# A decoder layer's prologue by tiles of 128 of the model width: x, adaLN weights and the first projections on one core

## The reference, cut to what matters

```python
mod = jax.nn.silu(c) @ w_ada + b_ada            # c (1, 1024), w_ada (1024, 3072)
shift, scale, gate = jnp.split(mod, 3, axis=-1)
h = x * (1.0 + scale[:, None, :]) + shift[:, None, :]
proj = h @ w_in + b_in                          # w_in (1024, 6664)
# split into sb_q, sb_k, sb_v, sb_z | ml_q ... ml_z | ml_i, ml_f (4 + 4 columns) | merge gates
```

## Time and profile before

| | us |
|---|---|
| median of 3 runs | 1022.5 (1020.33 to 1023.93) |
| the profiled execution | 1021.37 |
| its span, first to last instruction | 1019.6 |
| PE busy in the span | 955.2 (94%) |
| DVE busy | 600.2 (59%) |
| ACT busy | 456.5 (45%) |
| POOL busy | 177.3 (17%) |
| DMA | 73.64 MB, mean 72 GB/s |
| mean granted TensorE clock | 0.975 |

### The profile page before, as it was taken

One profiled execution on the slowest core, in us unless ns is written; L12 is line 12 of the kernel. 1 busy time (PEld: TensorE's weight loads), 2 busy tenths in 40 slices (PEclk: granted clock), 3 DMA queues, 4 the chain that ended last, 5 costly groups with the idle time before them and its releaser, 6 DMA issues.

```text
span 1019.6 us, 14219 instructions
## 1 busy us (share of the span) xinstructions
PE 955.2 (94%) x4965; PEld 765.9 (75%) x4965; DVE 600.2 (59%) x1100; ACT 456.5 (45%) x811; POOL 177.3 (17%) x145
## 2 busy tenths in 40 slices
PE   3399999999999999999999999999999999988995
PEld 2367877888877888778888778788788888866883
DVE  2854785665795655765648857543653332264766
ACT  1133465654465563656554656534743222251221
POOL 1101022322022330132420233211100000002220
PEclk9689998999999999999999999999999999999998
DMA  8702111111211102201112111125712211332232
GB/s 290 249 11 68 44 51 42 33 32 31 93 41 32 40 21 62 72 21 51 30 32 93 36 27 42 32 52 181 242 48 67 51 41 41 94 109 97 83 109 97
DMA packets 78083, 73.64 MB, mean 72 GB/s; under 512 B 4792, under 2 KB 66360, under 8 KB 78044
## 3 DMA queue, kind: packets, MB, share of 16 engines
q1 hardware_dynamic: 73116, 58.31, 20.0%
q0 software_dynamic: 2624, 8.54, 2.5%
q10 hardware_dynamic: 2304, 6.29, 1.6%
HBM read 64.59 MB, written 8.40 MB: 72 GB/s over the span
## 4 chain that ended last, share of the span: by engine, by line
PE 82%; DVE 10%; issue 2%; ACT 2%; DMA 2%; SPq 1%; POOL 0%; DVEq 0%; ACTq 0%; POOLq 0%
PE bank L618 42%; PE bank L598 9%; PE bank L599 9%; PE bank L600 9%; PE bank L731 3%; PE bank L715 3%; PE bank L704 1%; DVE m_q L1522 1%; DMA x_rows<-in_x 1%; DMA a_raw<-in_w_ada 1%; PE bank L744 1%; DVE a_acc L1295 1%; DVE m_q L1534 1%; DVE m_w L1546 1%; PE bank L687 1%
## 5 line engine op out<-in xcount | busy, mean ns | idle before, releaser
L618 PE MATMUL bank<-hH,wH 128*128 128x512 f32 x704 | 282.3, 401 | 0.7 <-DVE wL L1309 0.7
L618 PE MATMUL bank<-hL,wH 128*128 128x512 f32 x704 | 280.3, 398 | 0.0
L618 PE MATMUL bank<-hH,wL 128*128 128x512 f32 x704 | 276.2, 392 | 0.0
L557 POOL TENSOR_TENSOR ez<-ez,rem 128x512 f32<-128x512 f32 (+3 forms) x96 | 139.2, 1470 | 415.4 <-DVE rem L1471 415.4
L1309 DVE SCALAR_TENSOR_TENSOR wL<-w_raw,wH 128x512 fp32r<-128x512 f32 (+1 forms) x122 | 90.8, 748 | 150.7 <-ACT wH L896 149.9
L618 PEld LDWEIGHTS bank<-hH,wH 128*128 128x128 f32 x704 | 132.9, 189 | 39.9 <-issue 10.7
L618 PEld LDWEIGHTS bank<-hH,wL 128*128 128x128 f32 x704 | 133.1, 189 | 27.6
L618 PEld LDWEIGHTS bank<-hL,wH 128*128 128x128 f32 x704 | 133.1, 189 | 25.4 <-issue 1.0
L896 ACT ACTIVATE wH<-w_raw 128x512 fp32r<-128x512 f32 (+1 forms) x122 | 75.5, 620 | 108.7 <-PE bank L600 75.2
L1471 DVE TENSOR_TENSOR_SCAN rem<-rem,ones 128x512 f32<-128x512 f32 (+3 forms) x96 | 88.6, 965 | 39.0 <-ACT rem L981 39.0
L968 ACT ACTIVATE ez<-bank 128x512 f32<-128x512 f32 (+3 forms) x96 | 41.9, 489 | 97.2 <-PE bank L706 97.2
(11 more groups left out here) (234 smaller groups left out, 1458.3 us busy)
## 6 DMA issues: line engine op xcount, KB each, us to landing
w_raw<-in_w_in SPq DMA_DIRECT2D x104, 256.0 KB, 2.9
a_raw<-in_w_ada SPq DMA_DIRECT2D x16, 512.0 KB, 4.8
x_rows<-in_x SPq DMA_DIRECT2D x8, 512.0 KB, 7.2
raw<-in_w_ada POOLq DMA_DIRECT2D x8, 512.0 KB, 5.6
x_in<-in_x SPq DMA_DIRECT2D x8, 512.0 KB, 4.2
out_y<-res SPq DMA_DIRECT2D x8, 512.0 KB, 2.9
raw<-in_w_out SPq DMA_DIRECT2D x10, 256.0 KB, 4.5
m_w<-bm_scratch ACTq DMA_DIRECT2D x4, 512.0 KB, 4.3
```

The source lines that it names most:

```text
L557: g.tensor_tensor(e, e, r, ALU.mult).then_inc(a_done[h], 1)
L618: ins = t.matmul(proj_ps[half][:], w, a, start=(r == 0), stop=(r == JOB_MM // 2 - 1))
```

## The change

All loads of the prologue but the parameters are cut by 128 columns of the model width. For tile d SP loads a column block of x (`x_rows[:, :, cols_d]`, 1024 pieces of 512 bytes, 512 KB) and column blocks of the shift and scale parts of `w_ada` (two loads of 1024 pieces of 512 bytes). `a_raw` has 3 buffers of one tile each. Weight chunks 0 to 5 are now gate rows, q and k for tiles 0 to 3 (g = 0, 1, 2) and 4 to 7 (g = 3, 4, 5); their split parts have buffers of their own (`w_proH`, `w_proL`). Chunks 6 to 9 (v and z) are as they were.

Per tile d, DVE accumulates `ada_rows(d)` (8 instructions of 256 columns), PE sums (`ada_columns(d)`, 4 matmuls of one column), DVE makes the two columns of `mod`, PE transposes the x tile (`turn_x(d)`, 8 transposes), ACT reads the bank with scale and bias applied (`shifted(d)`, two instructions, and a third for `hH`), DVE makes `hL` (`low_h`, one iteration later), and PE adds the tile to gate rows, q and k (`tile_of`, 18 matmuls). DVE's old pass over `xT` and its copies out of PSUM are gone. Jobs v and z follow whole. The eight DMAs of the gate rows go from POOL to SP, behind the last prologue chunk. The pieces below belong to SP, to PE, to ACT and, the last two, to DVE:

```diff
+            for d in range(KT):
+                cols_d = slice(d * P, (d + 1) * P)
+                sp.dma_start(x_rows[:, :, cols_d], x_v[:, :, cols_d]).then_inc(x_cols_in[d], 16)
+                if d >= A_BUFS:
+                    sp.wait_ge(ada_used, KT * (d - A_BUFS + 1))
+                for what in range(2):
+                    sp.dma_start(a_raw[:, d % A_BUFS, :, what], w_ada_w[:, :, what, cols_d])\
+                        .then_inc(a_in[d % A_BUFS], 16)
+                if d == 0:
+                    for g in range(3):
+                        pro_load(g)
+                elif d < 4:
+                    pro_load(d + 2)
+            for g in range(PRO_CHUNKS, 2 * PRO_JOBS):
                 pro_load(g)
-            for n in range(2 * KT):
-                k, what = divmod(n, 2)
-                if n >= 4:
-                    sp.wait_ge(ada_used, n - 3)
-                sp.dma_start(a_raw[:, n % 4], w_ada_v[:, k, what * D:(what + 1) * D]).then_inc(a_in[n % 4], 16)
-            for g in range(3, 2 * PRO_JOBS):
-                pro_load(g)
+            sp.wait_ge(rows_zero, 5)
+            for half in range(2):
+                sp.wait_ge(drained[half], 1)
+            for q in range(4):
+                sp.dma_start(r_f[32 * q:32 * q + NH, :], r_if[NH:2 * NH, :]).then_inc(rows_in, 16)
...
+            ada_columns(0)
+            for d in range(KT):
+                turn_x(d)
+                if d:
+                    tile_of(d - 1, 0, PRO_K - 1)
+                if d + 1 < KT:
+                    ada_columns(d + 1)
+                if d:
+                    tile_of(d - 1, PRO_K - 1, PRO_K)
+            tile_of(KT - 1, 0, PRO_K)
+            pe.sem_inc(w_first_used, PRO_K)
+            for n in range(PRO_K, PRO_JOBS):
+                project(0, 0, JOB_MM, base_job=n, other_banks=1 if n == PRO_K else 0)
...
+            def shifted(d):
+                act.wait_ge(mod_done, 2 * d + 2)
+                if d > 1:
+                    act.wait_ge(hL_done, d - 1)
+                for n in range(2):
+                    act.wait_ge(m_filled[n], d + 2 - n)
+                    a.activation(h_raw[:, d % 2, halves(n)], misc_ps[n][:], ACT.Identity, scale=mod[:, 1, d:d + 1],
+                                 bias=mod[:, 0, d:d + 1]).then_inc(m_drained[n], 1)
+                for n in range(2):
+                    act.wait_ge(m_drained[n], d + 2 - n)
+                a.activation(hH[:, d], h_raw[:, d % 2], ACT.Copy).then_inc(hH_done, 1)
             for g in range(3):
                 pro_split(g)
             for d in range(KT):
-                act.wait_ge(h_full, d + 1)
-                a.activation(hH[:, d], xT[:, d], ACT.Copy).then_inc(hH_done, 1)
-                if d == 5:
-                    pro_split(3)
+                shifted(d)
+                if d < 6:
+                    pro_split(d + 3)
...
             for d in range(KT):
+                ada_rows(d)
+                mod_columns(d)
                 if d == 0:
-                    mod_columns(0, 0, ADA_FIRST)
-                if d == ADA_FIRST:
-                    mod_columns(1, ADA_FIRST, KT)
-                if d == 0:
-                    dve.wait_ge(m_drained[1], 8)
-                v.tensor_scalar(xT[:, d], xT[:, d], mod[:, 1, d:d + 1], mod[:, 0, d:d + 1], ALU.mult, ALU.add)\
-                    .then_inc(h_full, 1)
-                if d:
+                    for g in range(3):
+                        pro_split(g)
+                else:
                     low_h(d - 1)
-                if d == 6:
-                    pro_split(3)
+                if d and d < 7:
+                    pro_split(d + 2)
             low_h(KT - 1)
...
+            row_logs()
+            pro_split(PRO_CHUNKS + 3)
+            row_columns()
+            for g in range(2 * PRO_JOBS, 2 * PRO_JOBS + 2):
+                pro_split(g)
```

More of the change, by code:

```diff
@@ L124 @@
 PRE = 48
-ADA_FIRST = 3
+PRO_K = 3
+PRO_CHUNKS = 2 * PRO_K
+A_BUFS = 3
 def segments():
@@ L366, in build_kernel @@
         M_PRO, M_PER = [10, 9], [20, 20]
+        pro_ps = [[y_ps[0:2 * NH, :], misc_ps[2][0:2 * NH, :]],
+                  [proj_ps[half][:] for half in range(2)], [z_ps[half][:] for half in range(2)]]
+        ada_ps = misc_ps[0]
         F_V, F_MK, F_MV, F_CHUNK, F_HN = 0, 1, 2, 3, 19
@@ L641, in _, with ada_columns @@
-            for d in range(KT):
-                if d == 0:
-                    pe.wait_ge(ada_used, 2 * KT)
-                for what in range(2):
[L645 to L649, removed]
+            def ada_columns(d):
+                pe.wait_ge(ada_used, KT * (d + 1))
+                pe.wait_ge(m_drained[0], d + 1)
+                for what in range(2):
+                    for part in range(2):
+                        ins = t.matmul(ada_ps[:, what:what + 1], a_acc[:, d % 2, part, what],
+                                       ones[:, 0:1], start=part == 0, stop=part == 1)
+                ins.then_inc(ada_done, 1)
@@ new lines, in tile_of @@
+            def tile_of(k, first, last):
+                pe.wait_ge(hL_done, k + 1)
+                if k % 4 == 0:
+                    pe.wait_ge(wL_done, PRO_K * (k // 4 + 1))
+                for n in range(first, last):
+                    w = [z[:, PRO_K * (k // 4) + n, k % 4, 0:P if n else 2 * NH] for z in (w_proH, w_proL)]
+                    for half in range(2):
+                        ins = split_product(pro_ps[n][half], w, (hH[:, k, halves(half)], hL[:, k, halves(half)]),
+                                            k, KT)
+                        if k == KT - 1:
+                            ins.then_inc(filled[half], 1)
@@ L880, in _ @@
             a.preload_act_table_set("natural_log_exp_and_others")
[L883 to L889, removed]
+            act.wait_ge(cols_done, 1)
+            a.activation(small[:, 0:KT], cols[:, ROW_C:ROW_C + KT], ACT.Exp, scale=-1.0).then_inc(c_exp, 1)
             def split_high(slot, loads, freed, scale=1.0, width=P):
@@ L943, in _ @@
                     g = 2 * n + 3 + half
[L944 to L950, removed]
+                    if PRO_CHUNKS + 3 <= g < 2 * PRO_JOBS + 2:
+                        pro_split(g)
+                if n == 2:
                     act.wait_ge(rows_in, 16 * 8)
@@ L1285, in _, with ada_rows @@
             dve.wait_ge(silu_done, 1)
[L1287 to L1304, removed]
+            def ada_rows(d):
+                dve.wait_ge(a_in[d % A_BUFS], 32 * (d // A_BUFS + 1))
+                if d > 1:
+                    dve.wait_ge(ada_done, d - 1)
+                for k in range(KT):
+                    acc, row = a_acc[:, d % 2, k % 2], a_raw[:, d % A_BUFS, k]
+                    if k < 2:
+                        v.tensor_scalar(acc, row, silu_c[:, k:k + 1], None, ALU.mult).then_inc(ada_used, 1)
+                    else:
+                        dve.wait_ge(ada_used, KT * d + k - 1)
+                        v.scalar_tensor_tensor(out=acc, in0=row, scalar=silu_c[:, k:k + 1], in1=acc,
+                                               op0=ALU.mult, op1=ALU.add).then_inc(ada_used, 1)
             def split_low(slot, number, scale=1.0, width=P):
@@ L1313, in pro_split @@
             def pro_split(g):
[L1314 to L1318, removed]
+                if g < PRO_CHUNKS:
+                    n = g % PRO_K
+                    columns = P if n else 2 * NH
+                    dve.wait_ge(wH_done, g + 1)
+                    v.scalar_tensor_tensor(out=w_proL[:, g, :, 0:columns], in0=w_raw[:, g % 3, :, 0:columns],
+                                           scalar=SB_SCALE if n == 1 else 1.0, in1=w_proH[:, g, :, 0:columns],
+                                           op0=ALU.mult, op1=ALU.subtract).then_inc(wL_done, 1)
+                else:
+                    split_low(g % 3, g + 1)
```

125 lines of the change are left out of this document (50 added, 75 removed).

## The result

The changed kernel takes 1029.12 us (median of 10 runs, 1025.95 to 1031.51), the kernel before beside it 1021.21 (10 runs, 1018.53 to 1023.93): ratio 1.0077, 95% interval 1.0063 to 1.009. The forecast was 1012.5. Its profiled execution has a span of 1027.4 us, 7.8 more than before. Two launches of the kernel before that were timed beside the first four experiments were slow, 1210.28 and 2426.31 us; the ratios leave them out.

What follows compares the result with a forecast made beforehand. PE was taken as the bound, so an earlier prologue shifts everything: chunk 6 lands at 49.2, 28.7 to the last tile, 22.0 for v and z, `gate_columns` at 100.6 instead of 110.6, hence 1012.5 us; range 1006 to 1022.5.

Steps and rivals of the forecast that it cites:

- all behind it is unchanged and moves with it: Everything behind the start of `gate_columns` keeps its length, so that start's 10.0 us gain passes whole to the kernel.
- Who waits for whom: Prologue lists: ACT, then DVE, then PE wait for weight chunk 6, so streaming by tiles runs for tiles 0 to 3 only.
- The block: ACT's `pro_split(6)` behind `shifted(3)` waits for chunk 6 until 49.2 us; ACT idles near 9 us, PE from 43 to 53.
- The price of the loads: Prologue loads in 512-byte pieces run at 329 GB/s, so 13.89 MB up to chunk 6 take 42.2 us.
- The bound of 275: Lower bound on the load rate in GB/s: chunk 6 lands 8.3 us later, leaving a gain of 1.7 us.
- SP's own waits don't stretch it: SP's waits while issuing prologue loads don't delay chunk 6's landing at 49.2: each `ada_rows(1)` to `(4)` ends with two tiles queued.
- The rounds behind the block: DVE's rounds after chunk 6's splits: 6.1 us, then 7.1, with `ada_rows(7)` done at 66.6.
- 12 slow matmuls (5.1) ahead of its sums: In the second round after chunk 6, PE's lower-clock matmuls precede its sums, making that round 7.1 us.
- Rival 3: PE stays at the lower clock between the tile stage's short bursts: 16 us late, 1028 us; chance 0.04.
- The gate rows' path: Gate rows complete at 75.2, through bias, DMAs, Exp, Ln and `row_logs` to split 9 at 92.2; PE waits 0.7 us.
- rival 4: No stall in the prologue, or its gain eaten by hand-offs or load price: within 3 us of before; chance 0.12.
- the case of 395 GB/s: Prologue loads at big-piece rate: chunk 6 lands at some 44.5 us, limited by DVE's pace; gain 14.7 us.

Runs made afterwards that it cites:

- the first four experiments: Kernel before with 48 do-nothing instructions on PE, or 34 on DVE; changed kernel with PE's, or DVE's, loop head aligned: 1021.73, 1027.17, 1025.64, 1029.01 us.

## Why the prediction was wrong

It said 10 us faster, 0.73 on faster; the kernel is 8 us slower, outside the range. Two steps failed: "all behind it is unchanged and moves with it" (item 6, some 8 us), and the time of the last tile, which made the prologue's gain vanish (items 2 to 5, 9.9 us).

1. **Who waits for whom: right.** The block is where it was put, with its releasers, the idle stretch on PE and the fallen clock. Taking it away brought 16 us: the rounds of 5.96 us run on while the loads arrive, and PE keeps its clock.
2. **The price of the loads: mis-sized.** 329 GB/s came from a stretch of 1.5 us; steady, the stream gives 290. 13.89 MB at 290 are 47.9 us and not 42.2: 5.7 of the 7.0 us by which the block ended late. The bound of 275, which came from the packets' own busy time, was nearer than either direct rate.
3. **"SP's own waits don't stretch it": false.** It looked only at the `w_ada` buffers. Chunk 3's wait for DVE's first split held SP 3.6 us, and the rate from 15 to 20 us was 222 GB/s. What remains of the 7.0, 1.3 us, I put to this: 5 us at 222 and not at 290 lose 1.2. That share wasn't measured alone.
4. **The rounds behind the block: PE's part mis-sized.** The last `ada_rows` ends at 76.0, 19.8 after the block, where 17.4 were forecast. The steps on DVE were right (2.46 and 0.62 for `ada_rows`, 1.22 for `low_h`). Two terms of PE were not. "Four are 0.9" for `ada_columns` counts records as products: the 32 of the earlier trace rows are 16 sums, so four sums are 8 records and take 1.87 us at the lower clock, 0.95 at the upper. With that the first round took 6.8 and not 6.1. And the 7.1 of the second has "12 slow matmuls (5.1) ahead of its sums", while PE's list has 18 there and the transposes. The timeline of PE has the missing third of tile 3 from 62.21 to 64.92, then the transposes, then the 12:

```profile
62.21 0.77 PE L613 MATMUL bank<-hH,w_proH 128*128 128x512 f32 x1
...
64.92 1.91 PE L662 MATMUL bank<-ident,x_rows 128*128 128x128 f32 x8
66.48 0.78 PE L613 MATMUL bank<-hH,w_proH 128*8 128x512 f32 x1
...
70.17 0.95 PE L650 MATMUL bank<-ones,a_acc 128*128 128x1 f32 x8
```

   `ada_rows(6)` had ended at 67.25, so DVE waited for PE, and the round took 8.8. The clock was not the reason: it was back at about 68 us (0.50, 0.50 and 0.67 in the windows above), and the 12 matmuls took 3.7 us and not the 5.1 that the forecast had. Rival 3 had no part in it.
5. **From the last `ada_rows` on: half a us late.** It is 34.5 us to `gate_columns`, where 34.0 were forecast, and this is PE's: the 36 matmuls of tiles 6 and 7 took 8.45 us and not 8.1. The gate rows' path was 1.1 us longer than forecast up to Exp, since SP's eight small issues took 5.0 us and not 3.0, from 85.87 on:

```profile
85.87 2.58 SPq L458 DMA_DIRECT2D r_f<-r_if  x4
88.49 2.44 SPq L460 DMA_DIRECT2D r_i<-r_if  x4
```

   Split 9 ended at 101.96, and PE waited for it 0.55 us, where I had 0.7. That the two agree is luck: the sum of this path slipped (82.2 + 2.1 + 6.5 are 90.8 and not 91.5), and without the slip no wait was forecast.
6. **What the sum lacked: the returns.** Items 2 to 5 bring `gate_columns` from 100.6 to 110.5 (7.0 + 2.4 + 0.5), which is the time of rival 4, "no gain", though with the block in place. The step that turned that into a loss was "all behind it is unchanged and moves with it". The instructions are the same ones, but in another place of their lists, and that alone costs 8 to 9 us. Nothing in the sum priced the lists' length, though the page of before shows queues of kind instruction and the diff shows that both lists grow. With that cost taken away the changed kernel takes 1020.07 us: inside the stated range, but with a gain of 0.5 us and not of 10.
7. **A slip that decided nothing.** In the case of 395 GB/s, 38.5 + 3.4 + 1.9 are 43.8 and not 44.5.

## What to carry to other kernels

When a change adds instructions ahead of a long loop, compare the return of that loop in both traces (idle time ended by "issue", blocks in the queues of kind instruction) before judging the change itself: an alignment of the loop's head separates the two, and here it was worth 0.9%. Ask of each wait in a hand-written order what lies behind it in the same list: a split that isn't due for 30 us stood ahead of the tiles and cost 16 us. Price a stream by a row of the same kind that is long enough to be steady, and ask whether the engine behind it could use more: here PE's 5.96 us a tile was the pace once the block was gone. To find such a pace, look for the engine without idle time, not for the one with the longest list of steps: DVE has idle time in every round, and PE has none. And count a step's matmuls in the trace, not in the program: a plain float32 product stands there twice.

## What the runs showed of the hardware

- **A loop's return can cost 2.9 to 3.4 us on PE and 5.3 to 5.6 us on DVE**, while blocks of code are loaded (16 KB each for PE, 8 KB for DVE), and whether it does depends on where the head of the loop lies. 34 instructions that do nothing in DVE's list, or 80 in PE's, bring it about; 48 in PE's do not. With the head well placed a whole pass and its return run without any block being loaded (254 to 450 us in the kernel before). The Trainium skill (Runtime: NRT & Kernel Launch, Instruction fetch mechanics) says that a taken branch to a page outside the current window has to fetch it before going on. The trace agrees in kind; that the same loop with the same body returns without a gap from another place, it doesn't say. Why 48 is harmless and 80 is not stays open: only offsets by these counts and the aligned heads were run.
- **PE mostly pays more than the gap.** Behind five of the six gaps of PE in the three runs that have them, the next 48 matmuls take 12.59 to 12.80 us, against 10.93 without a gap; behind the sixth they take 11.16 and the clock stays at 1.00. A wait of 2.1 to 2.2 us for DVE was followed by the lower clock too, though not each time.
- **Pieces of 512 bytes, 4096 bytes or more apart, give 287 to 295 GB/s when the queue is full**; pieces of 4096 bytes give 399 in the same kernel as 290.
- **A small issue isn't cheap on SP:** the rows' DMAs took 0.61 to 0.65 us each to issue, a weight chunk 0.37. On POOL the rows' DMAs took 0.52 to 0.54.
